# Two transformer layers and a gated-delta tail on one core: the first two tiles behind each layer norm read x times the norm's weights, and the modulation rows get places of their own

## What is computed

```python
for l in range(DEPTH):                        # DEPTH = 2
    h = rmsnorm(x, attn_norm[l])              # x * rsqrt(mean(x*x) + eps) * weights
    z = h @ w_in[l]                           # four attention-like branches, gates
    ...
    x = x + merged @ w_out[l]
    h = rmsnorm(x, ffn_norm[l])
    u = causal_dwconv(h @ w_up[l], conv_w[l], conv_b[l])
    a, b = jnp.split(u, 2, axis=-1)
    x = x + (jax.nn.silu(a) * b) @ w_down[l]
```

## Time and profile before

| | us |
|---|---|
| median of 3 runs | 3021.63 |
| lowest and highest | 3019.94, 3023.08 |
| the profiled execution | 3025.86 |
| its span | 3024.0 |
| PE busy | 2932.3 (97%) |
| POOL busy | 1611.8 (53%) |
| DVE busy | 1560.6 (52%) |
| ACT busy | 738.2 (24%) |

### The profile page before, as it was taken

How to read it: one execution, slowest core, us unless ns; L and a number is a source line. 1 busy time by engine, 2 the same in 40 slices (tenths; PEclk the granted TensorE clock), 3 DMA queues, 4 the chain that set the end, 5 groups by cost and what they waited for, 6 DMA issues and landing times.

```text
span 3024.0 us, 41096 instructions
## 1 busy us (share of the span) xinstructions
PE 2932.3 (97%) x16398; PEld 2327.2 (77%) x16398; DVE 1560.6 (52%) x2926; ACT 738.2 (24%) x1574; POOL 1611.8 (53%) x1120
## 2 busy tenths in 40 slices
PE   9999999999999999999999999999999887999997
PEld 5777777777888877777777778888888676778886
DVE  4663452354887037543423548881252377777711
ACT  4333331112111023343321121121131223311110
POOL 4444455556555664345555565556535164566664
PEclk9999999999999999999999999999999999999999
DMA  5434444545776544344444456775534000355553
GB/s 208 153 128 144 154 149 165 172 149 189 249 247 235 193 164 169 127 140 150 149 164 171 151 187 241 264 244 179 175 123 139 1 3 23 112 181 195 192 192 138
DMA packets 133422, 491.97 MB, mean 163 GB/s; under 512 B 14816, under 2 KB 14816, under 8 KB 132336
## 3 DMA queue, kind: packets, MB, share of 16 engines
q1 hardware_dynamic: 70736, 261.91, 26.1%
q0 software_dynamic: 60912, 221.80, 20.6%
q10 hardware_dynamic: 1584, 5.63, 0.5%
HBM read 487.16 MB, written 2.13 MB: 162 GB/s over the span
## 4 chain that ended last, share of the span: by engine, by line
PE 75%; issue 7%; DVE 7%; POOL 7%; DMA 2%; ACT 1%; POOLq 0%; DVEq 0%; SPq 0%; ACTq 0%
PE dense L794 20%; PE dense L796 20%; PE dense L795 20%; POOL raw_lo L2712 4%; PE scores L1014 1%; PE scores L794 1%; PE scores L795 1%; PE scores L796 1%; PE O L1048 1%; PE O L1082 1%; PE turned L1036 1%; PE dense L1212 1%; DMA weights_hi<-stream 1%; PE scores L1068 1%; POOL weights_hi L2702 1%
## 5 line engine op out<-in xcount | busy, mean ns | idle before, releaser
L2712 POOL TENSOR_TENSOR raw_lo<-raw,weights_hi 128x1024 fp32r<-128x1024 f32 x423 | 1017.6, 2406 | 76.6 <-DMA weights_hi<-stream 34.5
L794 PE MATMUL dense<-h_hi,weights_hi 128*128 128x512 f32 x2192 | 873.9, 399 | 9.5 <-POOL raw_lo L2712 6.4
L796 PE MATMUL dense<-h_hi,raw_lo 128*128 128x512 f32 x2192 | 856.0, 390 | 0.0
L795 PE MATMUL dense<-h_lo,weights_hi 128*128 128x512 f32 x2192 | 854.3, 390 | 0.0
L2702 POOL DMA_DIRECT2D weights_hi<-stream x423 | 243.6, 576 | 1100.3 <-PE dense L796 996.9
L794 PEld LDWEIGHTS dense<-h_hi,weights_hi 128*128 128x128 f32 x2192 | 412.1, 188 | 124.0 <-issue 31.0
L796 PEld LDWEIGHTS dense<-h_hi,raw_lo 128*128 128x128 f32 x2192 | 411.7, 188 | 88.5
L795 PEld LDWEIGHTS dense<-h_lo,weights_hi 128*128 128x128 f32 x2192 | 412.6, 188 | 80.3
L794 PE MATMUL dense<-hidden_hi,weights_hi 128*128 128x512 f32 x528 | 206.4, 391 | 2.0 <-POOL raw_lo L2712 2.0
L795 PE MATMUL dense<-hidden_lo,weights_hi 128*128 128x512 f32 x528 | 206.1, 390 | 0.0
L796 PE MATMUL dense<-hidden_hi,raw_lo 128*128 128x512 f32 x528 | 206.0, 390 | 0.0
(11 more groups left out here) (433 smaller groups left out, 4537.8 us busy)
## 6 DMA issues: line engine op xcount, KB each, us to landing
raw<-stream SPq DMA_DIRECT2D x471, 512.0 KB, 3.6
weights_hi<-stream POOLq DMA_DIRECT2D x423, 512.0 KB, 4.7
decays<-stream ACTq DMA_DIRECT2D x8, 512.0 KB, 4.0
gates<-f_scratch SPq DMA_DIRECT2D x2, 1536.0 KB, 8.3
x<-x_in SPq DMA_DIRECT2D x2, 1024.0 KB, 7.6
cond_rows<-cond SPq DMA_DIRECT2D x2, 1024.0 KB, 6.9
dft<-dft SPq DMA_DIRECT2D x4, 512.0 KB, 4.8
out<-x SPq DMA_DIRECT2D x4, 512.0 KB, 2.6
```

The source lines that it names most:

```text
L794: nc.tensor.matmul(to, wh, xh, start=first, stop=False)
L795: nc.tensor.matmul(to, wh, xl, start=False, stop=False)
L796: return nc.tensor.matmul(to, wl, xh, start=False, stop=final)
L2712: nc.gpsimd.tensor_tensor(lo, src, hi, ALU.subtract).then_inc(weights_lo, 1)
```

## The change

Behind each of the four layer norms, the first two tiles no longer read the normalised h. ACT rounds `xT[:, k] * weights` (`gain_hi`) and DVE subtracts (`gain_lo`) as soon as chunk k of x is complete, so the blocks of these tiles don't need the row factor. PE does 4 blocks of them ahead of the statistics, 4 between statistics and row spread, and 8 behind it (at the start 8, 4 and 4); the idle products at these norms are taken out, and those at the start go from 42 to 30. The row factor is copied by ACT from `misc` to SBUF (`rows_sb`), and DVE multiplies the finished tiles in their banks by it (`scale_tile`), placed behind the fourth and the sixth scaling of `layer_norm`; ACT's evacuation of these tiles waits for it. From the third tile on h is read as before. In the attention norm h is written where the gained x lies, so DVE's scaling of chunk k also waits for PE's block k of the second tile. POOL takes two subtractions of weights around the power (`norm_between`).

The modulation rows leave the stream of weights: SP loads them into three places of their own (`load_ada`), behind the load of tile up f,1, waiting for the row three back; one or two rows in each of the steps 1 to 19, none in the last two. One of the places is where `tanh` lay; the tanh of the layers and of the tail's feed-forward part goes to the PSUM bank `O`, and the layers' `gate_out` to the bank `misc`. At the start SP loads the first half of x and the first weights, and the second half of x only when the first has landed. Some semaphores are shared; their counts are shifted.

```diff
-ADA_AFTER = [0] + [2 if f in (6, 12, 18) else 1 for f in range(1, FC)]
+ADA_STEPS = [0] + [2 if f in (2, 6, 10, 14, 18) else 1 for f in range(1, FC - 2)] + [0, 0]
...
+AFTER_CHUNKS = [(j, k) for n in range(2) for j in range(2) for k in range(4 * n, 4 * n + 4)]
...
-            sp.dma_start(xT[:, 4:8, :], x_in[:, 4:8, :]).then_inc(s_x[1], 16)
...
+            def load_ada(n):
+
+                if n >= len(ADA_AT):
+                    sp.wait_ge(ada_read, 2 * (n - len(ADA_AT) + 1))
+                sp.dma_start(ada_w[n % 3], ada_in[n]).then_inc(ada_landed[n % 3], 16)
...
-            sp.wait_ge(s_x[1], 16)
             for n, item in enumerate(DENSE.item_list):
+                if n == 1:
+                    sp.wait_ge(s_x[0], 16)
+                    sp.dma_start(xT[:, 4:8, :], x_in[:, 4:8, :]).then_inc(s_x[1], 16)
+                if n == 2:
+                    sp.wait_ge(s_x[1], 16)
                 load(n)
...
+                if item[0] < TAIL and item[1] == "up" and item[3]:
+                    for n in range(ADA_BEFORE[item[2]], ADA_BEFORE[item[2] + 1]):
+                        load_ada(item[0] * ADA_L + n)
...
-            for _ in range(42):
+            for _ in range(30):
                 nc.tensor.matmul(dense[:, 1, :], idle_src[:, 0:P], idle_src, start=True, stop=True)
...
+                fill(4)
+                if l == 0:
+                    pe.wait_ge(s_const, CONST_LANDED)
+                    fill(4)
                 norm_stats((l, 1))
...
+                fill(4)
                 norm_rows((l, 1))
-                idle_products(dense[:, 1, :], 12)
+                fill(8 if l else 4)
                 pre(l)
...
+                fill(4)
                 norm_stats((l, 2))
-                idle_products(dense[:, 1, :], 6)
+                fill(4)
                 norm_rows((l, 2))
-                idle_products(dense[:, 1, :], 12)
-                fill(FC * 2 * KC)
+                fill(FC * 2 * KC - 8)
...
             def result(key):
                 act.wait_ge(dense_mark, DENSE.out_mark[key])
+                if key in ROW_SCALED:
+                    act.wait_ge(row_scaled, ROW_SCALED[key])
...
+            def gain_hi(name, k):
+
+                nc.scalar.activation(gained_hi[name[1]][:, k, :], xT[:, k, :], ACT.Copy, scale=norm_gain(name, k)
+                                     ).then_inc(gained_hi_ready, 1)
...
+                if name in FIRST_TILES:
+                    act.wait_ge(rows_ready, number + 1)
+                    nc.scalar.activation(rows_sb, misc[:], ACT.Copy).then_inc(rows_copied, 1)
...
+            def scale_tile(name, j):
+
+                src, _ = result(FIRST_TILES[name][j])
+                nc.vector.tensor_tensor(src, src, rows_sb, ALU.mult).then_inc(row_scaled, 1)
...
                 for k in range(KC):
+                    if which == 1:
+                        dve.wait_ge(dense_mark, DENSE.read_mark[(l, k)])
                     norm_scale(name, k, lambda k: small[:, at + k:at + k + 1], hT, xT)
                     if k % 2:
                         split_lo_even(name, k - 1)
+                    if k in (3, 5):
+                        scale_tile(name, (k - 3) // 2)
...
+            def norm_between(name, w):
+
+                low(w)
+                issue(w + 1)
+                norm_pow(name)
+                low(w + 1)
+                issue(w + 2)
+                split_lo_odd(name)
```

More of the change, by code:

```diff
@@ L160, in __init__ @@
         for l in range(DEPTH):
-            walk(l, ("tok",), ("kIB",), order=AFTER_NORM)
+            walk(l, ("tok",), ("kIB",), order=AFTER_CHUNKS)
             for p in [("qI", 0), ("qI", 1)] + lead("A", 0):
@@ L197, in __init__ @@
         for n, (key, k, total, item, m) in enumerate(rows):
-            if key not in self.outs and key[1] != "ada":
+            if key not in self.outs:
                 self.outs[key] = len(self.outs)
@@ L225, in ffn @@
         first = int(l == TAIL)
-        walk(l, ("up", 0, first), ("up", 0, 1 - first), order=AFTER_NORM)
-        ada = [("ada", n) for n in range(ADA_L)] if l < TAIL else []
+        walk(l, ("up", 0, first), ("up", 0, 1 - first), order=AFTER_NORM if l == TAIL else AFTER_CHUNKS)
         for f in range(1, FC):
@@ L230, in ffn @@
                 walk(l, ("up", f, j))
-            for _ in range(ADA_AFTER[f]):
-                if ada:
-                    walk(l, ada.pop(0))
         for d in range(KC):
             walk(l, ("down", d))
-    @staticmethod
-    def split(item):
-        return item[1] != "ada"
 DENSE = Dense()
@@ L293 @@
           **{n: O_TAIL + i for i, n in enumerate(("X", "L", 3, 4, 5))}}
+FIRST_TILES = {(l, which): [(l,) + p for p in pair] for l in range(DEPTH)
+               for which, pair in ((1, (("tok",), ("kIB",))), (2, (("up", 0, 0), ("up", 0, 1))))}
+ROW_SCALED = {key: 2 * NORMS[name] + j + 1 for name, pair in FIRST_TILES.items() for j, key in enumerate(pair)}
+GAINED_HI_AT, GAINED_LO_AT, ROWS_AT = 42, 50, 95
 SPLITS = {(0, 1): 0, (0, 2): 1, (1, 1): 2, (1, 2): 3, "L": 4, 4: 5}
@@ L1654, in _ @@
                 if l == 0:
-                    for k in range(KC):
-                        act.wait_ge(s_x[k // 4], 16)
-                        nc.scalar.activation(first_squares[:, k, :], xT[:, k, :], ACT.Square).then_inc(squared, 1)
+                    for half in range(2):
+                        act.wait_ge(s_x[half], 16)
+                        for k in range(4 * half, 4 * half + 4):
+                            gain_hi((0, 1), k)
+                        for k in range(4 * half, 4 * half + 4):
+                            nc.scalar.activation(first_squares[:, k, :], xT[:, k, :], ACT.Square).then_inc(squared, 1)
                     act.dma_start(const[:, 0:at], const_in[:, 0:at]).then_inc(rope_landed, 16)
@@ L1690, in _ @@
                         act.wait_ge(up_gate, F)
-                    nc.scalar.activation(tanh_sb, side_a[half], ACT.Tanh, scale=0.5).then_inc(up_tanh, 1)
+                    nc.scalar.activation(up_tanhs, side_a[half], ACT.Tanh, scale=0.5).then_inc(up_tanh, 1)
             act.wait_ge(s_io, 16)
@@ L2165, in _ @@
                                     ).then_inc(s_init, 1)
[L2166 to L2172 removed]
+            for half in range(2):
+                dve.wait_ge(s_x[half], 16)
+                for k in range(4 * half, 4 * half + 4):
+                    gain_lo((0, 1), k)
+                for k in range(max(1, 4 * half), 4 * half + 4):
+                    dve.wait_ge(squared, k + 1)
+                    if k > 1:
+                        dve.wait_ge(square_added, k - 1)
+                    first, done = (first_squares[:, 0, :] if k == 1 else acc), (square_added if k < KC - 1 else first_added)
+                    nc.vector.tensor_tensor(acc, first, first_squares[:, k, :], ALU.add).then_inc(done, 1)
+            dve.wait_ge(s_const, CONST_LANDED)
             at = CONST_AT["ident"]
@@ L2267, in _ @@
                         elif j == 0:
-                            for n in range(sum(ADA_AFTER[:f]), sum(ADA_AFTER[:f + 1])):
+                            for n in range(ADA_BEFORE[f], ADA_BEFORE[f + 1]):
                                 ada_rows(l, n)
@@ L2272, in _ @@
                         dve.wait_ge(hidden_ready, F)
-                    nc.vector.scalar_tensor_tensor(out=gate_out, in0=tanh_sb, scalar=1.0, in1=side_a[half],
+                    nc.vector.scalar_tensor_tensor(out=gate_out, in0=up_tanhs, scalar=1.0, in1=side_a[half],
                                                    op0=ALU.add, op1=ALU.mult).then_inc(up_gate, 1)
@@ L2681, in _ @@
                 dve.wait_ge(hidden_ready, F)
-                nc.vector.scalar_tensor_tensor(out=gate_out, in0=tanh_sb, scalar=1.0, in1=side_b[half], op0=ALU.add,
+                nc.vector.scalar_tensor_tensor(out=grid_gate, in0=up_tanhs, scalar=1.0, in1=side_b[half], op0=ALU.add,
                                                op1=ALU.mult).then_inc(up_gate, 1)
@@ L2685, in _ @@
                 dve.wait_ge(up_gate, F + 1)
-                nc.vector.tensor_tensor(hidden[:, f, :], gate_out, src, ALU.mult).then_inc(done, 1)
+                nc.vector.tensor_tensor(hidden[:, f, :], grid_gate, src, ALU.mult).then_inc(done, 1)
                 evac_wait((TAIL, "up", f, 0))
```

143 lines of the change are left out of this document (76 added, 67 removed).

## The result

| | before | changed |
|---|---|---|
| median (lowest to highest), 4 runs each | 3020.78 (3019.39 to 3023.08) us | 3037.64 (3036.33 to 3038.66) us |
| ratio, 95% interval | | 1.0049, 1.0037 to 1.0062 |
| profiled execution, its span | 3025.86, 3024.0 us | 3036.33, 3034.5 us |

The changed kernel is slower by 0.49%, 16.9 us between the medians. No median or range in this document holds the one execution of the version with both causes joined that took 3279.07 us, at a mean granted clock of 0.84.

The account below looks back on a forecast made before the run. TensorE, busy 97% of the span, was taken as the bound. Start +3.4, layer 0 feed-forward +2.4, layer 1 attention +1.0 and feed-forward +2.3 made +9.1 us: 3035.0 profiled, 3030.7 us median; range 3018 to 3042.

Parts of the forecast that it names:

- The third tile's wait: Counted from t0, the last product's end before a norm: third tile at +23.3 or +19.6 us, PE idle 9.8 or 6.1.
- 4.7 us of saved time: Layer 0 feed-forward norm: PE's saved time and 4.0 us more turn into one wait of 9.8 us for a bank.
- rival (D): First tile evacuated before the rest of each norm, giving back 5.8 us per norm: 2991 us; chance 0.04, mixture 0.06 more.
- The clock: Behind PE's waits of 10, 6 and 10 us, products run at half clock: 2.0 us per norm, between 0 and 3.4.
- Rival (C): PE's clock never falls, or only where PE waits anyway: 3023 us; shares 0.27 for no change with a mild main forecast.
- Rival (B): PE's clock falls inside each norm as well, after 1.85 us of one-column matmuls; four times 2.5 us: 3041 us, chance 0.13.
- Part 2: Modulation rows in their own places: all ten PE pauses in the feed-forward parts go, minus 7.0 us (bound minus 5).
- The start: Second half of x at 12.8 us, statistics done 23.5, first tile evacuated 38.6, chain ending 57.8: +3.4 us (0 to +6).
- The attention norm of layer 1: Later third tile +0.3 and slow clock 2.0 us, less what the 0.65 us rope wait pays: +1.0 us.
- From span to median: Profiled execution forecast at 3035.0 us; median taken 4.2 us lower, as in the kernel before: 3030.7 us.

Follow-up runs that it names:

- both causes joined: Changed kernel with the first two tiles evacuated early, plus 10, 8, 8 and 8 idle products in the first wait behind each norm: 3020.68 us, again 3020.49 us.
- early order: Changed kernel with the first two tiles scaled and evacuated earlier and the condition's tanhs behind the first gate: 3016.52 us, again 3015.17 us.
- the version with idle products: Changed kernel with idle products (43, 32 and twice 54) in PE's waits for the third tile: 3031.11 us, ratio 1.0024.
- version with own places: Kernel before with modulation rows in three separate places and tanh and gate_out in PSUM; norms and start as before: 3015.93 us, again 3014.46 us.

## Why the prediction was right, and where its sizes were off

The changed kernel is slower, as forecast, at a time within the range and 7 us above the predicted one.

- **The third tile's wait is set by the evacuation of the first.** Right, by steps and in size: 23.3, 19.6 and 23.3 us from t0 predicted, 23.55, 19.67 and 23.55 measured; waits of 9.8 and 6.1 against 9.74 and 5.85; released by DVE side_a and by ACT's copy. The row spread at full clock: 0.75 predicted, 0.81 (724.85 to the next product at 725.66). The early order shows the cause on the chip: the same operations in another order give 20 us back. (The prediction's "4.7 us of saved time" should be 5.8, as its rival (D) has it; the sum uses neither.)
- **The clock.** Right for the waits taken together: 8.0 us predicted, 7.2 in four by count of slow products, though 1.0 to 2.4 each. With the clock kept the kernel lost 5.0 to 6.5 us of its time. Rival (C) is out for the changed kernel; the version with idle products is what it describes, and had 3031.11 for its 3023, as far off as the forecast itself. Rival (B) is out: the norm's own stretch has a granted clock of 1.00. The rule of the Trainium skill (TensorE: Matmul & The Clock Gate, Part 1), that the array's clock follows its recent activity, held where PE stood for 6 to 10 us, and was worth 5.0 to 6.5 us.
- **Part 2.** Right in size: -7.0 predicted, 7.6 and 8.0 us faster when measured alone. Between the traces the two feed-forward parts gave -2.6 and -3.7 for -3.6 and -3.4. One pause stayed. That the places, and not gate_out in PSUM, brought it is argued, not tested apart.
- **The start.** The term was too small: +3.4 predicted, +5.0 and +5.9. The second half of x was put at 12.8 us and ACT began on it at 13.38, the first tile opened at 15.91 (15.2 predicted); the sums, predicted to begin at 22.6 and to be over at 23.5, began at 24.31 after a wait of 0.74 us, since DVE's additions stood behind its own four subtractions, 4.85 us of them from 16.33 on, beside POOL's two of weights, 5.2 us from 13.43 on. Of these 1.7 us the later way to the third tile gave back 0.5 (39.78 for 38.6), and kA 0 opened at 59.31 and not 57.8.
- **The attention norm of layer 1.** The size (+1.0; +1.2 and +1.3) is right by luck. The slow stretch was 5 products, 1.0 us and not 2.0; the 0.65 us wait for DVE's rope, from which part of the loss was to be paid, is still there at 1131.78, so nothing was paid; and by the prediction's own numbers 0.3 + 2.0 - 0.65 would be 1.65 and not 1.0. In the first pair the 1.24 us are 0.24 of the later third tile and 1.0 of the clock.
- **From span to median.** This is the larger miss. The prediction took the distance between the profiled run and the median, 4.2 us, over from before to after. The profiled run of the changed kernel has no such distance: 3036.33, 1.3 under its median. Of the 4.2 us the second trace places 3.0 in norm L, in how early the half clock set in there; that most runs of before lack this loss is inferred from the eight of the thirteen traces that lack it. That the change between the first two traces, +10.5 us, lies near the predicted +9.1 is therefore partly luck: without that loss the first pair would have had about +13.5. Profiled run to profiled run the change is +10.5 us, 1.4 from the +9.1; median to median +16.9 and +13.2.
- **Rival (D)**, whose order the early kernel has, was mis-sized: 2991 us predicted, 3016.52 and 3015.17 measured. It took the third tile at +13.5 as the end of the matter. On the chip the tile opens at +15.40, after a wait of 1.59 us, and POOL's subtraction of the next weights, behind its share of the norm, costs another 2.04 us. And (D) counted 5.8 us for the start as well: against the version with own places the early order is 1.3 and 2.2 us later there in the two pairs of traces, 1.6 and 0.1 later at the feed-forward norm of layer 0, 0.0 and 0.4 at that of layer 1, and 1.3 and 1.9 us earlier at the attention norm.

## What to carry to other kernels

Work that is moved ahead of a norm on the tensor engine can only pay when the engines that empty its banks take it up early as well, and even then it brought nothing measurable here; with two or four banks in turn, write down when the first early tile is out, not when it is computed. Where a saving opens a long wait, count the clock behind it. And time two changes that come together one by one: here the whole gain was in the small one.

## What the runs showed of the hardware

- DVE's subtraction with two SBUF inputs (gained_lo) took 740 ns at least, 4432 in the median: where POOL works through operations of its own, DVE's ends only 0.6 us behind the last of them. Ahead of the norm this was hidden. Behind the feed-forward norm of layer 1 the same meeting lengthened PE's wait by 1.2 us in one of two traces. DVE and POOL of the changed kernel, ahead of the norm:

```profile
696.61 4.46 DVE L1950 SCALAR_TENSOR_TENSOR gained_lo<-x,small_sb,gained_hi 128x512 fp32r<-128x512 f32 x1
...
696.86 2.41 POOL L2781 TENSOR_TENSOR raw_lo<-raw,weights_hi 128x1024 fp32r<-128x1024 f32 x1
699.22 1.29 POOL L2799 TENSOR_TENSOR squares_sum<-squares_sum,squares 128x512 f32<-128x512 f32 x1
```

- Waits of 9.7 us were followed by 12 and 11 products at half clock and one of 5.85 us by 5, but in the second trace the 9.74 us by 5 and the 5.86 us by 9: the length of the slow stretch doesn't follow the length of the wait.
- 1.85 us of one-column matmuls between full products left the granted clock at 1.00, at the three norms that have them and in both traces of the changed kernel, where 2.73 us of four-column matmuls had been followed by half clock in the tail.
- The same program's traces differ by 3 us at norm L alone, through the moment at which the clock falls, and so do traces of different versions: a single profiled run doesn't carry a difference of 3 us.
